# Cache copies moved into the experts' loop of a hybrid decoder layer, with its sample softmax divided behind the values

## The reference

```python
q, k, v, u = split(rmsnorm(x) @ w_in)
o_a = dilated attention: keys at distances 0, d, 2d .. <= window,
      for (window, d) in (128,1), (512,4), (2048,16), with a position bias,
      merged by the softmax denominators
o_b = multi-scale pooling of u (means over 2/4/8/16 less the token) @ w_pool
x += [o_a | o_b] @ w_out
x += cross_attention(rmsnorm(x), memory)        # 4 heads of 256
x += top-4-of-32 experts: clamped SwiGLU of xb @ w_gate_up[e], then @ w_down[e]
y  = rmsnorm(x)
k_win_sample = concat(cache_k_win, k)[:, 4:]    # likewise v_win_sample
```

## Time and profile before

| | us |
|---|---|
| median of three runs | 1412.0 |
| the profiled execution | 1408.8 |
| its span, first to last instruction | 1406.9 |
| TensorE busy in it | 1260.8 (90%) |
| VectorE busy | 479.9 (34%) |
| ScalarE busy | 232.0 (16%) |
| GpSimd busy | 68.1 (5%) |

### The profile page before, as it was taken

The page is one execution under the profiler, slowest core; times in us unless marked ns, Lnnn a source line. Parts: engine busy times, 40 slices in busy tenths (PEclk is TensorE's granted clock), DMA queues, the critical chain, the costliest instruction groups (busy, mean ns, idle before and its releaser), DMA issues.

```text
span 1406.9 us, 16526 instructions
## 1 busy us (share of the span) xinstructions
PE 1260.8 (90%) x6407; PEld 530.5 (38%) x6407; DVE 479.9 (34%) x1033; ACT 232.0 (16%) x448; POOL 68.1 (5%) x69
## 2 busy tenths in 40 slices
PE   7988987988897999998999989999899999999986
PEld 5443333456644333332333323333333333333332
DVE  2367889332326412212232122321223212232124
ACT  1334343212311100110101100110011010011102
POOL 2000000005007000000000000000000000000000
PEclk9998988999997999999999999999999999999999
DMA  9999799999989899999999999999999999999993
GB/s 349 344 356 418 295 376 345 359 380 341 345 356 370 344 430 426 429 426 428 428 429 428 429 428 429 428 428 429 429 428 429 428 429 428 429 428 429 428 429 154
DMA packets 51740, 557.14 MB, mean 396 GB/s; under 512 B 7021, under 2 KB 9301, under 8 KB 15885
## 3 DMA queue, kind: packets, MB, share of 16 engines
q1 hardware_dynamic: 50629, 553.04, 96.1%
q0 software_dynamic: 1072, 3.57, 0.6%
HBM read 552.02 MB, written 71.72 MB: 443 GB/s over the span
## 4 chain that ended last, share of the span: by engine, by line
DMA 52%; PE 38%; DVE 7%; SPq 1%; issue 1%; ACT 1%; DVEq 0%; ACTq 0%; PEldq 0%
DMA wide<-in_w_gate_up 49%; PE bank L1926 12%; PE bank L1619 3%; PE bank L1639 3%; PE bank L1955 2%; PE bank L1721 2%; PE bank L1661 2%; PE bank L1484 2%; DMA wide<-in_cache_k_win 1%; PE bank L1552 1%; PE bank L1480 1%; DVE small L1153 1%; DMA slim<-in_w_xq 1%; PE bank L1709 1%; DVE wide L1150 1%
## 5 line engine op out<-in xcount | busy, mean ns | idle before, releaser
L1926 PE MATMUL bank<-wide,att 128*64 128x512 f32 x2048 | 463.3, 596 | 59.0 <-DMA wide<-in_w_gate_up 58.7
L1926 PEld LDWEIGHTS bank<-wide,att 128*64 128x64 f32 x2048 | 139.4, 136 | 362.9 <-issue 228.6
L1955 PE MATMUL bank<-slim,att 128*64 128x512 f32 x1024 | 226.8, 595 | 0.0
L1394 DVE TENSOR_SCALAR att<-bank 128x512 f32<-128x512 f32 x32 | 22.1, 692 | 469.6 <-PE bank L1926 469.6
L1955 PEld LDWEIGHTS bank<-slim,att 128*64 128x64 f32 x1024 | 70.6, 137 | 152.2 <-issue 149.2
L1373 DVE TENSOR_TENSOR x<-x,bank 128x512 f32<-128x512 f32 x68 | 46.6, 685 | 233.2 <-PE bank L1908 226.5
L962 ACT ACTIVATE att<-att 128x512 f32<-128x512 f32 x32 | 20.2, 632 | 518.0 <-DVE att L1394 518.0
L1908 PE MATMUL bank<-tb,att 128*128 128x512 f32 (+1 forms) x192 | 84.7, 611 | 1.8 <-ACT tb L971 1.3
L971 ACT ACTIVATE tb<-bank 64x512 f32<-64x512 f32 x64 | 37.9, 593 | 234.0 <-PE bank L1955 233.7
L1639 PE MATMUL bank<-slim,ta 128*128 128x512 f32 x128 | 60.6, 629 | 3.1 <-DVE wide L1151 3.1
L1153 DVE TENSOR_REDUCE small<-wide 128x24 f32<-128x1536 f32 x28 | 49.1, 1753 | 1.0
(11 more groups left out here) (289 smaller groups left out, 1153.7 us busy)
## 6 DMA issues: line engine op xcount, KB each, us to landing
wide<-in_w_gate_up SPq DMA_DIRECT2D x128, 2048.0 KB, 25.4
slim<-in_w_down SPq DMA_DIRECT2D x64, 2048.0 KB, 22.0
out_k_win_sample<-in_cache_k_win SPq DMA_DIRECT2D x16, 2044.0 KB, 20.4
out_v_win_sample<-in_cache_v_win SPq DMA_DIRECT2D x16, 2044.0 KB, 28.1
wide<-in_w_in SPq DMA_DIRECT2D x8, 1024.0 KB, 15.9
wide<-in_cache_v_win SPq DMA_DIRECT2D x8, 1024.0 KB, 5.5
wide<-in_cache_mem_k SPq DMA_DIRECT2D x8, 1024.0 KB, 23.9
wide<-in_cache_mem_v SPq DMA_DIRECT2D x8, 1024.0 KB, 14.3
```

The lines of the kernel that those rows point to most:

```text
L1926: ins = M(bk[half[h], :], rows[:, k, :], wide[:, k, c:c + 512], start=False, stop=k == KC - 1)
L1955: ins = M(bank_y[half[h], :], aT[:, f % 4, f // 4, :], slim[:, f, 512 * h:512 * h + 512], start=f == 0, stop=f == KC - 1)
```

## The change

1. The copies. The value caches of samples 6 and 7 (8.37 MB, four pieces) leave the list. SyncE issues them in the experts' loop, in eight quarters of a sample's cache (1.05 MB, 64 packets of 16,352 bytes), one behind the down weights of each of experts 1 to 8 (the second to the ninth). `COPIES` has other numbers (28 in all, so `copy(len(pieces))` issues none); the first burst is of 4 instead of 7.
2. The sample's softmax. GpSimd's sum over partitions, VectorE's sum, its reciprocal over 32 columns and its multiply are gone. TensorE adds the exponentials up itself (16 products with a column of ones into `sx_bank`), VectorE takes the reciprocal of one column, and ScalarE multiplies it in when it copies the values' result out (`keep`). The whole result is kept; `turn_values` picks each head's columns with 8 products and a smaller constant `own`.
3. The prompt's share. VectorE only takes the reciprocal (`unit_sum`), ScalarE multiplies (`unit_share`).
4. The first sample's keys go into `tb` and `mkT` instead of `slim`, so that six of the eight parts of `w_xk` can be fetched early; the key windows of samples 1 and 2 are fetched earlier; the four pool products move behind the transposes of the memory; the first key product of round 1 moves ahead of the first logits.
5. In ScalarE's rounds `sample_exp` and `late_values` stand ahead of `sample_out`, and in the last round ahead of `unit_out`.

```diff
-        COPIES = [7, 1, 1, 1, 1, 2, 1, 2, 2, 2, 3, 2, 1, 3]
+        COPIES = [4, 1, 3, 1, 1, 2, 2, 2, 2, 1, 3, 2, 1, 3]
...
+        LATE_COPIES = 6
...
-                for h in range(2):
+                for h in range(0 if b >= LATE_COPIES and dst == "v_win_sample" else 2):
...
+            slim_first(range(6))
             copy(COPIES.pop(0))
 
+            sp.wait_ge(w_read, 3)
+            window(kwin[1], i["cache_k_win"], 1, k_in[1])
             sp.wait_ge(w_read, 5)
-            window(kwin[1], i["cache_k_win"], 1, k_in[1])
+            window(kwin[0], i["cache_k_win"], 2, k_in[0])
...
             step0()
             copy(len(pieces))
-            with sp.Fori(1, EXPERTS) as e:
+            def late_copy(b, c):
+                dst, src = (ap.rearrange("b s h d -> b (s h d)").rearrange("b (c j a n) -> b c a j n", c=4, a=16, j=4)[ds(b, 1), c].rearrange("b a j n -> (b a) j n")
+                            for ap in (o["v_win_sample"][0, :, 0:KEEP], i["cache_v_win"][0, :, DEC_T:PAST]))
+                sp.dma_start(dst, src).then_inc(stored["copies"], 16)
+
+            LATE = 4 * (DEC_B - LATE_COPIES)
+            with sp.Fori(0, DEC_B - LATE_COPIES) as m:
+                for c in range(4):
+                    step(m * 4 + (c + 1), m * 4 + (c + 1))
+                    late_copy(m + LATE_COPIES, c)
+            with sp.Fori(LATE + 1, EXPERTS) as e:
                 step(e, e)
...
+            def unit_share(u):
+                nk = P * (UNITS[u][1] + 1)
+                act.wait_ge(rsum, u + 1)
+                for h in range(2):
+                    c = 10 + 4 * (u % 2) + h
+                    ins = A(lg[u % 2][:, h, 0:nk], lg[u % 2][:, h, 0:nk], ACT.Copy, scale=stat[:, c:c + 1])
+                ins.then_inc(scaled, 1)
+
+            def keep(b):
+                if b:
+                    b_, use = place(("pvt", b - 1))
+                    act.wait_ge(bank_full[b_], use + 1)
+                act.wait_ge(rz_in, b + 1)
+                ps, s = product(act, "pv", b)
+                A(kept, ps[:, :], ACT.Copy, scale=rz[:, b:b + 1]).then_inc(s, 1)
...
             def values(b):
-                pe.wait_ge(prob, b + 1)
+                pe.wait_ge(sexp, b + 1)
+                pe.wait_ge(rz_in, b)
...
+                for kind in range(4):
+                    for t in range(DEC_T):
+                        n = NS if kind == 3 else P
+                        M(sx_bank[32 * t:32 * t + 32, b:b + 1], flat[0:n, kind, :], ones[0:n, 0:1], start=kind == 0, stop=kind == 3,
+                          tile_position=(0, 32 * t))
...
-                for c in range(4):
-                    ins = M(ps[:, 4 * c:4 * c + 4], kept[:, P * c:P * c + P], own[:, AW:AW + DEC_T], start=True, stop=True)
+                for h in range(HEADS):
+                    ins = M(ps[64 * (h % 2):64 * (h % 2) + 64, 4 * (h // 2):4 * (h // 2) + 4], kept[:, HD * h:HD * h + HD],
+                            own[:, DEC_T * h:DEC_T * h + DEC_T], start=True, stop=True)
```

More of the change, by code:

```diff
@@ L293, in build @@
                 add(*f)
+        for g in range(4):
+            add("pool", g)
         for b in range(1, DEC_B):
@@ L512, in _ @@
             sp.wait_ge(cleared, 1)
[L513 removed]
+            src = i["cache_k_win"][0, 0]
+            sp.dma_start(near_first, src[PAST - 512:PAST].rearrange("(p t) h d -> p t (h d)", p=P)).then_inc(k_in[0], 16)
+            far = src.rearrange("(p t) h d -> p t (h d)", p=P)[0:96, 0:4, :].rearrange("(g r) t n -> r g t n", r=3)
+            for r in range(3):
+                sp.dma_start(far_first[r:P:4], far[r]).then_inc(k_in[0], 16)
             b, use = place(("tr1", 2, 1))
@@ L803, in _ @@
             turned_in(2), turned_in(0)
-            act.wait_ge(loaded["pscale"], 16)
-            for g in range(4):
-                ps, s = product(act, "pool", g)
-                A(tb[:, 4 + g, :], ps[:, 0:T], ACT.Copy, scale=pscale[:, g:g + 1]).then_inc(s, 1)
+            late_keys(1)
             rows_out(1)
@@ L1135, in keep, with part_of_sum, unit_sum, row @@
-            def keep(b):
+            def part_of_sum(b):
+                b_, use = place(("pv", b))
+                dve.wait_ge(bank_full[b_], use + 1)
+                V.reciprocal(rz[:, b:b + 1], sx_bank[:, b:b + 1]).then_inc(rz_in, 1)
+            def unit_sum(u):
+                c = 10 + 4 * (u % 2)
+                dve.wait_ge(expd, 2 * u + 2)
+                V.reciprocal(stat[:, c:c + 2], stat[:, c:c + 2]).then_inc(rsum, 1)
+            def row(b, t):
+                kw, pd = kwin[b % 2], prod if b else prod_first
+                ps, s = product(dve, "qb", b, t)
@@ L1175, in _ @@
             dve.wait_ge(loaded["toep"], 16)
-            for g in range(4):
-                b_, use = place(("pool", g))
-                dve.wait_ge(bank_full[b_], use + 1)
+            dve.wait_ge(stored["pool"], 48)
+            dve.wait_ge(k_in[1], 64)
+            dve.wait_ge(late_k, 2)
+            row(1, 0), shift(0)
             logits(0)
             for b in range(1, DEC_B):
-                dve.wait_ge(expd, 2 * b)
-                share(b - 1, b, P * (UNITS[b - 1][1] + 1))
+                if b > 1:
+                    unit_sum(b - 1)
                 dve.wait_ge(k_in[b % 2], 64 * (b // 2 + 1))
                 dve.wait_ge(late_k, b + 1)
-                for t in range(DEC_T):
+                for t in range(0 if b > 1 else 1, DEC_T):
                     row(b, t)
-                    if t < 3:
-                        (shift, sums, shares)[t](b - 1)
-                    if b >= 2 and t == 0:
-                        keep(b - 2)
+                    if b == 1 and t == 1:
+                        unit_sum(0)
+                    if b > 1 and t == 0:
+                        shift(b - 1)
+                        part_of_sum(b - 2)
                     if t == 2:
@@ L1535, in _ @@
             turn_rows(0)
-            pe.wait_ge(loaded["wpool"], 16)
-            for g in range(4):
-                pe.wait_ge(pooled, g + 1)
-                ps, s = take(pe, "pool", g)
-                M(ps[:, 0:T], wpool[:, g, :], dT[:, g, :], start=True, stop=True).then_inc(s, 1)
             def row(b, t):
@@ L1559, in _ @@
                     row(0, t)
+            row(1, 0), row(1, 1)
             turn_rows(1)
@@ L1675, in _ @@
                     fill(f)
+            pe.wait_ge(loaded["wpool"], 16)
+            for g in range(4):
+                pe.wait_ge(pooled, g + 1)
+                ps, s = take(pe, "pool", g)
+                M(ps[:, 0:T], wpool[:, g, :], dT[:, g, :], start=True, stop=True).then_inc(s, 1)
             for b in range(1, DEC_B):
```

121 lines of the change are left out of this document (60 added, 61 removed).

## The result

The changed kernel takes 1433.2 us (median of 4 runs, 1432.7 to 1433.8), the kernel before 1412.0 (4 runs, 1402.6 to 1412.2). The ratio is 1.0164, with a 95% interval of 1.0136 to 1.0191: slower, as forecast, by 21 us where 17 were predicted. (The prediction adds 20.0 us to the profiled 1408.8 and is then laid beside the median of 1412.0; that is where the 17 come from.) The profiled execution has a span of 1431.5 us against 1406.9, 24.6 us more, to be laid beside the 20.0.

A forecast was written before the change was run, and what follows sets the result against it. Transfers at 428 GB/s bound the experts' loop; compute up to 465 us sets its start. Profiled 1408.8 + 19.6 for the copies + 0.4 lost in the front = 1428.8, predicted 1429; range 1412 to 1441, 8 times in 10.

The forecast's parts named there:

- The bound: Experts' loop: end set by when expert 1's weight fetch begins (465.47 us), plus remaining bytes at 428 GB/s, plus 27 us.
- The copies: Experts' loop: four pieces (8.37 MB) moved in from ahead of it cost 19.6 us at 428 GB/s.
- the rival with 1414: Before the loop: the three pieces held back expert 1's first weights, so only 4.9 us is added; chance 0.08.
- The rival of a slowed TensorE: Experts' loop: copies also slow TensorE by waits or a clock fall, giving 1437 us; chance 0.10.
- The front: Everything ahead of the experts: gains and losses sum to -0.4 us, so experts start about when they did.
- The sums: Attention rounds on TensorE: 16 one-column sums, 32 instructions, add 1.3 us a round, 2.7 at half clock.
- a round with two pieces can't be under 18.4 us: Late attention rounds: transfer floor (4.19 + 3.67) / 0.428; three such rounds in a row cap the gain at 2.1 us.
- start and rounds: Attention: +2 us for an earlier start and +2.5 us over five rounds.
- The end of attention: First output projection: ScalarE's last prompt-output copy waits behind the last value window; loss 3 to 7.3 us, taken 6.
- The cross query weights: Cross query product: one piece less and an emptier queue give back up to 2.4 us, taken 2.4.
- Rounds at full clock: Attention: rounds run at full clock down to the transfer floor, copies still paid, 1418 us; chance 0.15.
- VectorE alone paces: Attention: less VectorE work saves 2.8 us a round, 30 us in the front altogether, 1398 us; chance 0.05.

The follow-up runs named there:

- run 1: Kernel before, with only the last four pieces moved into the experts' loop as eight quarters, attention as before: 1429.3 us, ratio 1.0155.
- run 2: Changed kernel without the eight copies in the loop, leaving 8.37 MB uncopied: 1413.5 us.
- run 4: Changed kernel with ScalarE's last attention round in the earlier order, sample_out and unit_out ahead of the last exponentials and value rows: 1423.1 us, ratio 1.0106.
- run 3: Changed kernel with the four pieces back behind expert 0's down weights and no copy in the loop: 1419.6 us, ratio 1.0079.
- run 8: Changed kernel with the sums over the probabilities made three times in a row: 1440.9 us.
- run 7: Changed kernel with one piece instead of two in attention rounds 4, 5 and 6, three pieces queued ahead of the cross query weights: 1431.5 us, ratio 1.0149.
- run 10: Changed kernel with run 3's and run 4's edits, plus TensorE's sums before the value-window wait and late rows third: 1405.6 us, ratio 0.9961.
- run 12: Run 10's kernel with ScalarE's copy of the turned values ahead of the late value rows in every round: 1402.2 us, ratio 0.9954.
- run 9: Changed kernel with run 3's and run 4's edits, one piece in rounds 4 to 6, the three pieces spread elsewhere: 1414.6 us, ratio 1.0033.

## Why the prediction was right, and where it was off

**The bound: right.** Fetching starts when compute lets it, and the bytes behind it pass at 428 GB/s; runs 1 and 2 move the end by bytes only. From the fetch to the end of the span it is 961.9 us in the changed kernel, 961.3 in run 1 and 963.5 in run 4, all with the eight quarters, and 941.4 before and 943.1 in run 2 without them.

**The copies: right.** Foretold 19.6 us; the pitch gives 19.4, run 2 gives 19.7, run 1 gives 17.7 by medians and 19.5 by spans. The three pieces in the hole were free (run 1), so the rival with 1414 is out; four pieces there cost 2 to 6 us (run 3). The trace does not agree with the 358 GB/s of the Trainium skill (DMA: Bandwidth & Descriptors, "Where 436 GB/s comes from"): by it the copies would have cost 23.4 us, an estimate. The rival of a slowed TensorE is out too: clock 1.00, and nothing beyond the bytes.

**The front: wrong by 3.8 us, which is nearly the whole miss.** Foretold was -0.4 us, a loss of 0.4 at the fetch; measured was a loss of 4.2. Term by term:
- The sums: right in kind, too dear. 0.47 us by run 8 at full clock, 0.64 at the lower one, where 1.3 was taken. That is 15 to 20 ns an instruction.
- The turned output takes 0.64 us where 1.2 was taken, the share's wait 1.14 to 1.45 where 1.45 was.
- Each late round should then have gained about 1.7 us instead of 0.3, and run 7 shows that it can. What took it is the step "a round with two pieces can't be under 18.4 us, which caps the gain at 2.1". The floor was priced at the loop's 428 GB/s, though the earlier trace rows gives 360 for this very stage. In the changed kernel 374 GB/s pass from 185.44 to 228.86 us, and 7.86 MB / 0.374 is 21.0 us; from projection to projection the late rounds take 20.9, 20.9 and 22.5. The gain at the start of the values went 1.6, 3.0, 3.5, 5.5 us over the first four rounds and then back, 3.8, 2.9, 1.5. With ScalarE's order mended (run 4) the first projection starts 3.8 us sooner than before, where start and rounds had been put at 4.5: the sum came out nearly right, by two errors against each other.
- The end of attention is the step that failed in size: "loss between 3 and 7.3 us, taken 6". The wait was foretold, and the projection did begin 6.0 us later than before, at 261.25. But this time already holds what the rounds had gained: once the projection waits for a value window, they are no longer a gain of their own, and -6 could not stand beside +2.5 and +2. Counted properly the order cost 9.8 us (run 4), and 2.1 us of lower clock behind the idle time were not in the sum at all.
- The last sample's sums cost 0.5, not 1.3. So far 3.8 - 9.8 - 2.1 - 0.5 = -8.6, and the cross query product begins at 311.77 against 303.36, 8.4 later.
- The cross query weights gave back 1.0 us, not 2.4. "Stood" was misread: of the 2.4 us in the earlier trace rows TensorE worked 1.69 and waited 0.72. The end of the product tells the price: 343.05 against 335.62, 7.4 later.
- A term that the sum did not have: cross-attention gave back 3.0 us. The counterparts of the earlier trace rows in the changed kernel:

```profile
311.77 31.28 PE L1774 MATMUL bank<-ta,slim 128*128 128x288 f32 x128 [0.90 <-DVE ta L1074]
344.10 1.07 PE L1785 MATMUL bank<-att 128*32 128x256 f32 x16 [1.05 <-DVE att L1284]
```

  Behind the product TensorE waits 1.05 us for VectorE instead of 1.88, then 1.58 instead of 2.15, and two groups of transposes take 0.66 and 1.91 us instead of 1.11 and 3.12, at a granted clock of 1.00 where it had been 0.57 (350 to 354 us). No run tells why the clock had fallen just there.
- Together -8.6 + 1.0 + 3.0 = -4.6, against the 4.2 measured at the fetch. That the total came so near is in part luck: by the terms that the sum had, rightly sized, the fetch would be 7 to 8 us late, and the 3.0 us of cross-attention, which it did not have, brought that back.

**The rivals.** Rounds at full clock: in part. The values of the third round take 2.78 us where they took 5.2, those of the fourth to seventh 4.1 to 5.4, and the transfers held the rounds back anyway. VectorE alone paces: out; taking its work away brought 3.8 us at the first projection, not 28.

**The point on the weight loads.** The Trainium skill (TensorE: Matmul & The Clock Gate, "LDWEIGHTS (loading the stationary operand)") gives 0.85 us for the 32 instructions, an estimate. The trace's 0.47 at full clock does not agree with it; it is under it and under the row that was used.

## What to carry over

Behind a point where transfers are the bound, price a moved transfer by its bytes and ask what the place it left was worth: four pieces cost 19.7 us in the loop and 2 to 6 in a hole ahead of it. Where a term pins an operation to the arrival of a transfer, the gains ahead of it must not be added: take the later of the two times. A floor made of bytes must be worked out at the rate of its own stage, and a wait for a short copy is read from what stands ahead of that copy in its engine's list (runs 10 and 12). A gain at one point is not yet a gain at the end: runs 7, 9 and 10 start the first projection sooner than their comparison and give most or all of it up again behind it, in part to a lower granted clock.

## What the hardware showed that was not expected

- A window's time from issue to landing depends on what is still under way when it is issued. The value window lands after 5.5 us when it finds the queue empty (run 7) and after 10 us when two pieces are under way (the changed kernel; the pieces take 20.8 us from issue to landing, though one alone takes 13.5).
- The instructions of products over one column with 32 weight columns follow each other every 15 ns at full clock (1.40 us for 96, run 8).
- An idle time can cost more than its length. Both in the changed kernel and in run 4 the granted clock is 0.66 from 240 to 250 us, between the levels of 1.2 and 2.4 GHz. In run 4 TensorE is busy for 9.5 of the next 10 us and the clock is 1.00; in the changed kernel it is busy for 2.3 of them, and the clock is 0.76 and then 0.73. The projection behind takes 2.1 us more.
